# A hand-planned transformer layer on eight cores: other landing times in its planner, more staging room for first-use weights, fewer convolution items early, and another order of the first loads

## What is computed

```python
u = layer_norm(x) * (1 + scale) + shift          # scale, shift, gate from c @ w_ada
q, k, v, z_a, bg, cg, xin, z_c = split(u @ w_in) # eight projections, 1024 wide each
# 8 heads, two 64-wide score maps each, causal, with a relative-position bias
a = softmax(q1 @ k1.T + bias) - lam * softmax(q2 @ k2.T + bias)
o = rms_norm(a @ v) * subln_gain * (1 - lambda_init)
y_attn = o * silu(z_a)
y_conv = bg * causal_conv3(cg * xin) * silu(z_c)
g_a, g_c = split(sigmoid(u @ w_gate + b_gate))
merged = g_a * (y_attn @ w_branch[0]) + g_c * (y_conv @ w_branch[1])
out = layer_norm(ALPHA * x + (1 + gate) * (merged @ w_out)) * ln_gain + ln_bias
```

## Time and profile before

| | us |
|---|---|
| median of 3 runs | 3782.14 (3781.57 to 3782.67) |
| time of the profiled execution | 3780.95 |
| its span on core 4, first to last instruction | 3779.4 |
| spans of the other cores | 3717.2 to 3777.7 |

### The profile page before, as it was taken

The page is one execution under the profiler, slowest core; times in us unless marked ns, Lnnn a source line. Parts: engine busy times, 40 slices in busy tenths (PEclk is TensorE's granted clock), DMA queues, the critical chain, the costliest instruction groups (busy, mean ns, idle before and its releaser), DMA issues.

```text
span 3779.4 us, 69113 instructions; the slowest of 8 cores (3717.2 to 3779.4 us)
## 1 busy us (share of the span) xinstructions
PE 3535.4 (94%) x18328; PEld 1332.6 (35%) x18328; DVE 2680.9 (71%) x5121; ACT 2513.7 (67%) x2947; POOL 182.6 (5%) x229
## 2 busy tenths in 40 slices
PE   6899978899998899999999999999999999999997
PEld 2343323333333333333333333333333333333333
DVE  4346857688676966868777787577876876876875
ACT  1345656676777656776777776676777777777771
POOL 1000000000000000000000000000000000000000
PEclk7888889999999999999999999999999999999998
DMA  9758797898688876567655575555555655745644
GB/s 228 195 160 207 205 224 176 176 224 195 165 209 218 245 178 138 136 137 200 156 146 135 146 187 123 130 140 147 167 132 142 179 127 139 185 128 137 174 116 112
DMA packets 413573, 629.63 MB, mean 167 GB/s; under 512 B 143595, under 2 KB 177515, under 8 KB 409740
## 3 DMA queue, kind: packets, MB, share of 16 engines
q1 hardware_dynamic: 413196, 625.21, 66.0%
HBM read 521.38 MB, written 103.67 MB: 165 GB/s over the span
## 4 chain that ended last, share of the span: by engine, by line
PE 73%; DMA 12%; issue 4%; ACT 4%; DVE 4%; SPq 2%; POOL 0%; DVEq 0%; ACTq 0%; POOLq 0%
PE ps L29 73%; ACT PBT L43 3%; DMA ST<-wpk 3%; DMA TH<-rho_scr 3%; SPq L160 2%; DMA TH<-s_scr 1%; DMA rho_scr<-HS 1%; DVE QST L48 1%; DMA q_scr<-QB 1%; DMA BIG<-w_ss 1%; DMA s_scr<-HS 0%; DMA kT_scr<-KS 0%; PE ps L33 0%; DMA Q<-q_scr 0%; DVE PBT L48 0%
## 5 line engine op out<-in xcount | busy, mean ns | idle before, releaser
L43 ACT ACTIVATE PBT<-ps 128x1024 bf16<-128x1024 f32 (+1 forms) x2112 | 2018.5, 1009 | 675.1 <-PE ps L29 574.4
L29 PE MATMUL ps<-PBT,V 128*128 128x512 bf16 (+6 forms) x4608 | 1250.9, 365 | 91.2 <-ACT PBT L43 50.9
L29 PE MATMUL ps<-BIG,W 128*128 128x512 bf16 x4800 | 1272.8, 383 | 17.8 <-DVE BIG L48 6.5
L48 DVE TENSOR_TENSOR QST<-PBT 128x1024 bf16<-128x1024 bf16 x896 | 615.6, 687 | 399.1 <-ACT PBT L43 390.4
L29 PE MATMUL ps<-Q,K 64*128 64x512 bf16 (+6 forms) x4608 | 655.0, 365 | 15.2 <-ACT PBT L43 8.2
L29 PEld LDWEIGHTS ps<-BIG,W 128*128 128x128 bf16 x4800 | 455.1, 98 | 601.3 <-issue 121.8
L29 PEld LDWEIGHTS ps<-PBT,V 128*128 128x128 bf16 x4608 | 359.6, 98 | 768.4 <-issue 661.7
L48 DVE TENSOR_TENSOR QST<-QST 128x1024 bf16<-128x1024 bf16 x840 | 576.5, 686 | 37.0 <-DVE QST L48 0.9
L29 PE MATMUL ps<-UT,W 128*128 128x512 bf16 x1344 | 364.6, 400 | 9.4 <-ACT QB L43 2.4
L29 PEld LDWEIGHTS ps<-Q,K 64*128 64x128 bf16 x4608 | 146.5, 94 | 477.6 <-issue 463.8
L29 PE MATMUL ps<-W,UT 128*128 128x512 bf16 x896 | 240.0, 391 | 19.2 <-ACT W L43 17.7
(11 more groups left out here) (115 smaller groups left out, 1917.6 us busy)
## 6 DMA issues: line engine op xcount, KB each, us to landing
W<-w_bf SPq DMA_DIRECT2D x680, 256.0 KB, 4.1
V<-v_scr SPq DMA_DIRECT2D x288, 256.0 KB, 4.3
K<-kT_scr SPq DMA_DIRECT2D x288, 256.0 KB, 5.3
ST<-wpk SPq DMA_DIRECT2D x128, 512.0 KB, 7.9
X<-x_all SPq DMA_DIRECT2D x52, 512.0 KB, 6.9
w_bf<-W SPq DMA_DIRECT2D x104, 256.0 KB, 8.9
TH<-rho_scr SPq DMA_DIRECT2D x64, 256.0 KB, 8.9
TH<-s_scr SPq DMA_DIRECT2D x64, 256.0 KB, 7.5
```

The lines of the kernel that those rows point to most:

```text
L29: return lambda e: e.matmul(out(), lhsT(), rhs(), start=start, stop=stop)
L43: return e.activation(out(), in_(), func, **kw)
L48: return lambda e: e.tensor_tensor(out(), in0(), in1(), op)
```

## The change

In the planner, the two latencies are replaced by a table over three phases of the plan's time (before 180 us, to 1450 us, after) and kinds of transfer: 9.0 us for the 256 KB broadcasts; 5.0, 7.0 and 3.5 us for the 4 KB ones; 5.5, 9.0 and 5.5 us for 512 KB; 4.5, 8.5 and 4.0 us for stores; 5.0, 7.0 and 4.5 us for the rest. The setup's first-use weights get four more staging buffers in BIG 0 and 1 (pool PST0), and wait for the landing of `w_ss[5]` in the place of `modc`; the weights of the v units come in two halves among the loads of tile 0. The items of stages 2 to 6 get four more staging buffers in UT (pool PST2), and their loads wait for the evacuation of q unit 4 of the next tile. There are 3 buffers KS in the place of 2, 4 QB in the place of 2, 7 HS in the place of 8. `nslots` of stages 2 and 3 is taken times 0.8, and `NE` is 2 in the place of 5. (`SEQ["stk"]` is only a new name for a list, since `SEQ["st"]` now holds the staging pool.)

```diff
@@ -192,9 +192,19 @@
 
 def simulate(g, nunits=200):
     LAT = 0.14
-    DLAT = 4.5
-    CLAT = 5.5
     BW = 240e3
+
+    def dlat(o, t):
+        ph = 0 if t < 180.0 else 1 if t < 1450.0 else 2
+        if o.prio == 0 and o.nbytes == 1 << 18:
+            return 9.0
+        if o.prio == 0 and o.nbytes == 4096:
+            return (5.0, 7.0, 3.5)[ph]
+        if o.nbytes == 1 << 19:
+            return (5.5, 9.0, 5.5)[ph]
+        if o.prio >= 3:
+            return (4.5, 8.5, 4.0)[ph]
+        return (5.0, 7.0, 4.5)[ph]
     owner, lastvb = {}, {}
     freed = {}
     evs = []
@@ -271,7 +281,7 @@
         elif e == "sp":
             free[e] = t + d
             st["dma"] = max(st["dma"], t + d) + o.nbytes / BW
-            o.end = max(t + d + (CLAT if o.prio == 0 else DLAT), st["dma"] + 2.5)
+            o.end = max(t + d + dlat(o, t), st["dma"] + 2.5)
         else:
             free[e] = t + max(0.05, d - (0.1 if e == "act" else 0.084 if e == "dve" else 0.0))
             o.end = t + d
@@ -606,8 +616,8 @@
         PSM = mkpool("SM", 6, [128, 16])
         UT = sb("UT", [128, 8, 2, 8, 64], BF16)
         BIG = sb("BIG", [128, 4, 8, 512], BF16)
-        PBIG = Pool("BIG", [(("BIG", i),) for i in range(4)], [BIG[:, i] for i in range(4)])
-        PUT = Pool("UT", [tuple(("UT", i) for i in range(8)), (("BIG", 2), ("BIG", 3))],
+        PBIG = Pool("BIG", [(("BIG", i, 0), ("BIG", i, 1)) for i in range(4)], [BIG[:, i] for i in range(4)])
+        PUT = Pool("UT", [tuple(("UT", i) for i in range(8)), tuple(("BIG", i, o) for i in (2, 3) for o in range(2))],
                    [UT[:], BIG[:, 2:4].rearrange("p a b c -> p (a b c)").rearrange(
                        "p (k o t s) -> p k o t s", k=8, o=2, t=8)])
         PUT1 = Pool("UT", PUT.units[:1], PUT.aps[:1])
@@ -615,8 +625,8 @@
         PK = mkpool("K", 4, [128, 1024], BF16)
         PV_ = mkpool("V", 4, [128, 8, 128], BF16)
         PQ = mkpool("Q", 3, [128, 512], BF16)
-        PKS = mkpool("KS", 2, [128, 8, 2, 64], BF16)
-        PQS_ = mkpool("QB", 2, [128, 512], BF16)
+        PKS = mkpool("KS", 3, [128, 8, 2, 64], BF16)
+        PQS_ = mkpool("QB", 4, [128, 512], BF16)
         PVS = mkpool("VS", 3, [128, 512], BF16)
         PBT = sb("PBT", [128, 8, 2, 512], BF16)
         PPB = Pool("PB", [(("PB", i),) for i in range(8)], [PBT[:, i] for i in range(8)])
@@ -624,7 +634,7 @@
         PQS = Pool("QS", [(("QS", i),) for i in range(7)], [QST[:, i] for i in range(7)])
         POE = mkpool("OE", 3, [128, 2, 512])
         PTH = mkpool("TH", 4, [128, 512], fifo=False)
-        PHS = mkpool("HS", 8, [128, 24])
+        PHS = mkpool("HS", 7, [128, 24])
         PON = mkpool("ON", 2, [128, 512], BF16)
         TAT = sb("TAT", [128, 7, 528])
         PTA = Pool("TA", [(("TA", i),) for i in range(7)], [TAT[:, i] for i in range(7)])
@@ -634,6 +644,9 @@
                    list(PX.aps) + [PBT[:, i:i + 2].rearrange("p a b c -> p (a b c)").bitcast(F32)
                                    for i in (0, 2, 4, 6)] +
                    [QST[:, i:i + 2].rearrange("p a b c -> p (a b c)").bitcast(F32) for i in (0, 2, 4)])
+        PST0 = Pool("ST0", list(PST.units) + [(("BIG", i, o),) for i in range(2) for o in range(2)],
+                    list(PST.aps) + [BIG[:, i, 4 * o:4 * o + 4].rearrange("p a b -> p (a b)").bitcast(F32)
+                                     for i in range(2) for o in range(2)])
         PVS0 = Pool("VS0", list(PVS.units) + list(PON.units) + list(PQS_.units),
                     list(PVS.aps) + list(PON.aps) + list(PQS_.aps))
         PKS0 = Pool("KS0", list(PKS.units) + [(("LG", i),) for i in range(4)],
@@ -647,6 +660,9 @@
         POE0 = Pool("OE0", list(POE.units) + [(("TA", i), ("TA", i + 1)) for i in (0, 2, 4)],
                     list(POE.aps) + [TAT[:, i:i + 2, 0:512] for i in (0, 2, 4)])
         utf = UT[:].rearrange("p k o t s -> p k (o t s)").bitcast(F32)
+        utw = UT[:].rearrange("p k o t s -> p (k o t s)").bitcast(F32)
+        PST2 = Pool("ST2", list(PST.units) + [(("UT", 2 * i), ("UT", 2 * i + 1)) for i in range(4)],
+                    list(PST.aps) + [utw[:, 1024 * i:1024 * (i + 1)] for i in range(4)])
         PSTASH = Pool("STASH", [(("UT", i),) for i in range(8)] + list(PXN.units),
                       [utf[:, i] for i in range(8)] + [a.bitcast(F32) for a in PXN.aps], fifo=False)
 
@@ -693,7 +709,7 @@
 
                 def wv(n, w=w):
                     return lambda: w.ap().rearrange("p a b -> p (a b)").bitcast(F32)[:, n * 512:(n + 1) * 512]
-                g.dma((lambda w=w: w.ap().rearrange("p a b -> p (a b)").bitcast(F32)), A(w_ss[k]), writes=[(w, 0)],
+                g.dma((lambda w=w: w.ap().rearrange("p a b -> p (a b)").bitcast(F32)), A(w_ss[k]), writes=[(w, 0), ("ada", k)],
                       prio=1, nbytes=1 << 20)
                 for n in range(4):
                     g.op("pe", 0.9, MM((lambda vb=rows_[n]: bank[vb.ap()][0:1, :]), A(ccol[:, k:k + 1]), wv(n),
@@ -732,9 +748,10 @@
                  [(xb, 0), (sm, 2), (sm, 3)], [(xn, 0)], pr)
             return xn
 
-        def ln_tile(j):
-            SEQ["xn", j] = [ln_block(x_all[(8 * j + t) * 128:(8 * j + t + 1) * 128, :], 2 if j < 2 else 6, PX0 if j < 2 else PX)
-                            for t in range(8)]
+        def ln_tile(j, ts=range(8)):
+            SEQ.setdefault(("xn", j), []).extend(
+                [ln_block(x_all[(8 * j + t) * 128:(8 * j + t + 1) * 128, :], 2 if j < 2 else 6, PX0 if j < 2 else PX)
+                 for t in ts])
 
 
 
@@ -746,8 +763,8 @@
             uses[u] = n = uses.get(u, 0) + 1
             first = 2 if name[0] in ("k", "v", "q") else 1
             if n <= first:
-                s_ = VB(PST)
-                g.dma(s_.ap, A(wpk[u]), reads=[("modc", 13)], writes=[(s_, 0)], prio=2, nbytes=1 << 19)
+                s_ = VB(SEQ.get("st", PST))
+                g.dma(s_.ap, A(wpk[u]), reads=[SEQ.get("after", ("ada", 5))], writes=[(s_, 0)], prio=2, nbytes=1 << 19)
 
                 if name[0] == "wo":
                     def v2(f):
@@ -873,7 +890,7 @@
                 vb = mm8(wcol(w), (lambda k, uT=uT: (lambda: uT.ap()[:, k, 0].rearrange("p t s -> p (t s)"))),
                          lambda k: [(w, 0), (uT, k, 0), (uT, k, 1)])
                 qs = VB(PQB0 if j < 2 else PQS_)
-                fevac(qs.ap, bf(vb), [(vb, 0)], [(qs, 0)], scale=0.125)
+                fevac(qs.ap, bf(vb), [(vb, 0)], [(qs, 0), ("qe", j, m)], scale=0.125)
                 g.dma(A(q_scr[j, m]), qs.ap, reads=[(qs, 0)], writes=[("q", j, m)], prio=3, nbytes=1 << 17)
 
 
@@ -1400,7 +1417,9 @@
         nslots = [8 * (8 * j + 5) for j in range(NT)]
         kvq = [(16 * 0.24 + 40 * 1.724) if 1 < j < NT - 1 else 0.0 for j in range(NT)]
         nslots[0] = nslots[1] = 0
-        NE = 5
+
+        nslots[2], nslots[3] = 0.8 * nslots[2], 0.8 * nslots[3]
+        NE = 2
         ab_total = NT * 80 * 1.75 - (24 + 3 * (8 - NE)) * 1.75
         lo, hi = 0.0, 3.0
         for _ in range(50):
@@ -1414,10 +1433,13 @@
         SEQ["wide"] = True
         masks()
         ada()
-        ln_tile(0)
+        SEQ["st"] = PST0
+        ln_tile(0, range(4))
+        vw = [v_weights(0)]
+        ln_tile(0, range(4, 8))
+        vw.append(v_weights(1))
         ln_tile(1)
         lam()
-        vw = [v_weights(0), v_weights(1)]
         for j in range(2):
             if j == 1:
                 SEQ["wide"] = False
@@ -1429,6 +1451,7 @@
         for m in range(8):
             k_group(m, (0, 1))
             q_group(m, (0, 1))
+        SEQ["st"] = PST
         late_consts()
         ab = []
         for j in range(NT):
@@ -1457,10 +1480,13 @@
                 for m in range(8):
                     q_group(m, (j + 1,))
             left += budget[j]
+            if 1 < j < NT - 1:
+                SEQ["st"], SEQ["after"] = PST2, ("qe", j + 1, 4)
             while ai < len(ab) and left > 0 and (ab[ai][1] != "B" or ab[ai][0] < j):
                 left -= ab[ai][2][0]
                 ab[ai][2][1]()
                 ai += 1
+            SEQ["st"], SEQ["after"] = PST, ("ada", 5)
             p1 = g.filtime
             sl = SEQ["slots"]
             for i in range(s0, len(sl)):
```

More of the change, by code:

```diff
@@ L953, in attention @@
                                 pair_add(qa, pbs[si - 1], pb)
-                                SEQ["st"] = SEQ.get("st", []) if si > 1 else []
-                                stk = SEQ["st"]
+                                SEQ["stk"] = SEQ.get("stk", []) if si > 1 else []
+                                stk = SEQ["stk"]
                                 stk.append(qa)
```

## The result

The changed kernel takes 3671.73 us (median of 4 runs, 3665.07 to 3672.86) against 3782.4 for the kernel before (median of 4 runs): a ratio of 0.9702 with a 95% interval of 0.9685 to 0.9718, or 110.7 us less. The forecast was 3706, the range 3660 to 3775; the change is 1.46 times the 76 us of the sum. In some executions of every kernel here two or more cores are at 0.81 of the clock for longer, and the time is 1.5 to 16% above that of the others; all medians and ratios are of the others.

The account below looks back on a forecast made before the run. The prediction took PE, the busiest engine, as the bound, with only its 244.7 us of idle time and the clock to win. Setup 12, 310 to 1440 us 45, later 5, tail 14 sum to 76 us: 3706 us, range 3660 to 3775.

Parts of the forecast that it names:

- my forecast: Whole kernel: the terms come true as summed, 3706 us, own range 3680 to 3735; chance 0.45.
- all of it: Rival: PE's idle share from 310 to 1440 us falls to that of the later part, 135 us won, 3647; chance 0.12.
- 310 to 1440 us: Five edits shorten waits of ACT and DVE, so PE idles less: 45 us won, bounds 0 and 103.7.
- after 1440: 1440 to 3690 us: the plan now knows the broadcast takes 9.0 us; 5 us won, bounds 11 lost and 30 won.
- setup 12: Before 180 us: v weights load and are cast earlier, first half tile ends near 104 or 105: 12 us won.
- tail 14: After the last head: held-back fillers cover PE's 12.1 us gap, 12 us, plus 3 of clock less 1: 14 us.
- Byte-bound: Rival, 310 to 1440 us: DMA share of 0.84 to 0.90 is the limit; 45 and 5 not won, 3756; chance 0.22.
- The 11 us for store buffers: 310 to 1440 us: more QB and KS buffers, with their waits halved on PE, win 11 us.
- Step (3): 310 to 1440 us: the landing-time table puts operations after a broadcast or staging load later, behind ready work; no separate size.
- the 27 units: Stage 4: 27 of the 80 first-use units move there from earlier stages and cost 11 us against the gain.
- Bursts: Rival, first-use stretches: six staging loads in flight delay small transfers and K and V loads; 36 us lost, 3792; chance 0.10.
- The clock rival: Denser PE prolongs 0.81 past 490 us: 76 us eaten if held to about 1000, 3848 if to 1440; chance 0.06.

Follow-up runs that it names:

- its rows for the chain alone: Changed kernel with the table's rows for the head's chain (priority 0) and 4.5 us for every other transfer: 3671.1 us, ratio 0.9655 to the kernel before, third chip.
- the plan with 0.141: Changed kernel with the planner's semaphore latency 0.141 us in place of 0.14, which only gives another order: 3684.9 us, ratio 0.9695 to the kernel before, third chip.
- the factor 0.7: Changed kernel with nslots of stages 2 and 3 times 0.7 in place of 0.8: one run, 3669.9 us, third chip.

## Why the prediction was right, and where it was not

**Size.** The measured 110.7 us lie in the range and between "my forecast" and "all of it". The terms came out so, first on the slowest core and then on core 3, which was not at 0.81: 310 to 1440 us, 45 forecast, 41.8 and 28.9 of idle time; after 1440, 5 forecast, 18.3 and 8.4; setup 12, see below; tail 14, see below. The sum had 73 us of idle time and 3 of clock. Measured are 62.4 and 47.6 on the slowest core, 47.4 and 11.0 on core 3. So the idle time was forecast 11 to 26 us too large, and that the result lies beyond the sum and not below it is owed to the clock, which was not foreseen: to that extent the forecast was lucky.

**The step that was missing.** Apart from 3 us in the tail I priced the clock at nothing in the sum, and as a rival only in the other direction: a denser PE would prolong 0.81. Of the 110 us on the slowest core 47.6 are busy time, that is, clock. At most 29 of them come from the time at 0.81, 260 us on the core that set the time before and 110 on the one that set it after; the forecast was 0.81 on core 4 until about 480 again, and core 4 had none. The rest is fewer stretches at a lower clock still, which went with the idle time, also on core 3 and on the chips where no core was at 0.81. The earlier trace rows had the first part in them: two cores 61.8 us apart with one program. Where a slowest core is slow by clock, a change of any kind can move that term either way.

What decides which cores go to 0.81 stays open. It came in pairs (2b and 2b+1, which share a sequence) in every profile that had it. It came to six cores in the kernel before, to six with the new setup alone, to two or none in the changed kernel and its variants on the first two chips, to none with the table alone or with its rows for the chain alone, and to four in each of the profiles of the plan with 0.141 and of the factor 0.7. The rival's price of 0.15 us for each us at 0.81 was near: at most 0.19.

**Setup.** The forecast was that the second half tile's transposes start near 105 us and the casts' waits fall below 7. Timeline of core 0, changed kernel:

```profile
75.36 5.18 SPq L160 DMA_DIRECT2D BIG<-wpk  x4
...
84.43 0.68 DVE L737 BATCH_NORM_STATS2 SM<-QST 128x6 f32<-128x512 f32 x1
84.43 3.02 PE L29 MATMUL ps<-W,UT 128*128 128x512 bf16 x6 [4.76 <-ACT W L43]
...
104.81 1.95 PE L33 MATMUL ps<-ident,XN 128*128 128x128 bf16 x32
```

They start at 104.81 for 117.32, the first load is issued at 75.36, not 73, and the waits PE<-ACT W are 6.8 us. The size was right though the step to it ("six can be in flight") was not: there were four. What of the lead lasts to the end isn't shown: 4 us when it is undone, 12 between two medians whose interval includes none.

**310 to 1440 us.** Right in size on the slowest core, too large on core 3, and the order of the causes was partly wrong. Byte-bound does not hold from 480 us on: from 480 to 600 the slowest core's PE is idle 13.9 us and not 26.4 at a share of 0.91 and 0.90, and from 1020 to 1260 11.8 and not 30.9 at 0.92 and 0.89. From 310 to 480, at a share of 0.88 to 1.00, nothing was won, so there it isn't refuted. The 11 us for store buffers measured 6 or, by ratio, none: within chance. The two largest parts were the table (39 us) and the factor 0.8 (18 to 38), which I had listed as two of five with one answer; the staging in UT gave 14 or 7. By time the undone parts add up to 39+28+14+4 and 6+6 = 97 us, with 91 won on that chip; by ratio they are 36+18+7+4-4+4 = 65, so that the sum closes is no evidence. Step (3), that waits after a broadcast end here because the plan knows their landing time, fell for this stretch: without the table they are nearly as short.

**After 1440 us.** The mechanism was right and its size too small: 18.3 us on the slowest core and 8.4 on core 3 for 5. The old latencies bring back the wait for TH<-rho_scr and 16 to 19 us of PE's idle time, on the cores where the broadcast lands late. The 11 us that the 27 units were to cost against it did not come as forecast: their staging loads were all issued by 1391.3 us, and the share where I put it near 0.6 was 0.82 (1260 to 1440 us, core 0).

**Tail.** Right in mechanism: the gap is gone. 106 more matmuls between the last head's ACT step into TH and the end of `late` cost 8.1 us more instead of 106 times 208 ns = 22.0, which is the 14 us forecast. Undoing NE alone cost 6 or 4, within chance: the plan without it had a gap of 10, not 12.1 us, and lost no clock.

**Rivals.** Bursts did not happen: the items' staging loads now land after 11.2 us (before 800) and 12.1 us (after) against 9.4 and 8.5, longer than feared (about 10), yet on no core did PE wait for K or V between 310 and 1440 us. Only from 310 to 480 us, where the k, v and q units are at their second use and the share is 1.00 on core 3, is PE idle longer than before, by 8 us on that core, which is this rival's direction. The clock rival was the right subject with the wrong sign.

## What to carry to other kernels

When the slowest of several cores runs the same program at a lower clock, split its time into idle time and busy time before costing anything, and put what the low clock may give or take into the range. Cost the change on more than one core: of cores that were not at 0.81, two gained 58 us on one chip and two 69 and 77 on another, there even without the setup's part. When a plan has landing times, read them core by core: here the table was worth 19 us of PE's idle time after 1440 us on a core where the broadcast lands after 7.9 us, and the wait it is to end was under 3 us on cores where it lands after 4 to 5. In a list-scheduled kernel, look at which buffer each load really got: a pool that is named first may be held by an early load with no dependency. And before believing a few us between two plans, run a plan that differs by nothing, on the same chip as the kernel itself.

## What was not expected of the hardware

The clock of 0.81 came to pairs of cores and not to dies. In most profiles it lasted 110 to 270 us, began in the dense stretches before 500 us and was absent after 1440, where PE is 98% busy. But not in all: with the setup alone cores 2 and 3 had it again near the end, and in the profiled execution of the plan with 0.141 (3807.3 us) cores 4 and 5 were at it for 750 us from 3030 us to the end and cores 6 and 7 for 780 us between 100 and 1000. The Trainium skill ("TensorE: Matmul & The Clock Gate", Part 1) has the value, 13/16, and says that a whole die goes to it. The traces agree in the value and not in the die: in the kernel before, between 200 and 280 us, cores 0, 1, 4 and 5 were at 0.81 and the other four at 1.00, so two cores of each die had it and two had not.

Landing times differ by pair too: with the old latencies the 256 KB broadcasts landed after 7.3 to 7.9 us on cores 2 and 3 and after 4.0 to 4.9 on the six others, from 1440 to 3500 us, with one program.

The same kernel took 3782, 3724 and 3799 us on three chips, 2% apart, and the change was worth 3.0% on the first and 2.3% on the second.
